# Where the second homes of the activations begin: a shift of 32 columns instead of 48

## What is computed

```python
def mixer(h, hc, lp, rope, n_rows, need_ctx):
    f, nq, nk, nv, cq, ckv, kr, g = jnp.split(h @ lp['w_in'], IN_OFFSETS, axis=-1)
    ...
    out = merge_branches([y_f, y_na, y_mla], g, lp['w_branch'], lp['w_out'])
def swiglu(h, w_gate, w_up, w_down):
    return (jax.nn.silu(h @ w_gate) * (h @ w_up)) @ w_down
def sq_relu_mlp(h, w1, w2):
    u = jax.nn.relu(jnp.einsum("bsd,df->bsf", h, w1))
    return jnp.einsum("bsf,fd->bsd", u * u, w2)
```

## Time and profile before

| | us |
|---|---|
| median of 3 runs | 2148.93 |
| lowest, highest | 2146.88, 2150.05 |
| profiled execution | 2151.08 |
| its span, first to last instruction | 2149.2 |
| TensorE busy | 1972.9 |
| VectorE busy | 1300.5 |
| ScalarE busy | 847.9 |
| GpSimd busy | 138.9 |

### The profile page before, as it was taken

How to read it: one execution, slowest core, us unless ns; L and a number is a source line. 1 busy time by engine, 2 the same in 40 slices (tenths; PEclk the granted TensorE clock), 3 DMA queues, 4 the chain that set the end, 5 groups by cost and what they waited for, 6 DMA issues and landing times.

```text
span 2149.2 us, 31676 instructions
## 1 busy us (share of the span) xinstructions
PE 1972.9 (92%) x12304; PEld 1616.3 (75%) x12304; DVE 1300.5 (61%) x2152; ACT 847.9 (39%) x1364; POOL 138.9 (6%) x118
## 2 busy tenths in 40 slices
PE   4999989999988999999699898989997789988998
PEld 2776657646667788888578483779996789987998
DVE  5422464564447567768733557576667877777765
ACT  4422253253124222222523444454445754444444
POOL 0000000000030000303000000020111300000000
PEclk9999999999999999999899799999998899999999
DMA  8642512204552565565454240666552446653653
GB/s 303 207 137 79 176 40 79 64 1 161 192 172 97 182 212 180 189 202 192 150 196 157 79 142 1 232 212 204 196 192 92 140 148 206 194 165 99 196 188 125
DMA packets 280756, 332.04 MB, mean 154 GB/s; under 512 B 13190, under 2 KB 229692, under 8 KB 280508
## 3 DMA queue, kind: packets, MB, share of 16 engines
q1 hardware_dynamic: 268608, 323.05, 45.5%
q10 hardware_dynamic: 12028, 7.32, 1.3%
HBM read 329.31 MB, written 1.05 MB: 154 GB/s over the span
## 4 chain that ended last, share of the span: by engine, by line
PE 75%; DVE 9%; issue 5%; DMA 5%; ACT 4%; POOL 1%; SPq 1%; ACTq 0%; DVEq 0%; POOLq 0%
PE ps L546 20%; PE ps L547 19%; PE ps L548 19%; PE ps L1269 3%; PE ps L1295 2%; DVE SL L507 2%; PE ps L367 2%; PE ps L1279 2%; DMA RAW<-in_w_in 2%; DMA RAW<-in_w_out 1%; ACT SH L501 1%; PE ps L1504 1%; DMA EARLY<-in_w_mod 1%; DVE RSTD L988 1%; DMA RAW<-in_w_branch 1%
## 5 line engine op out<-in xcount | busy, mean ns | idle before, releaser
L507 DVE TENSOR_TENSOR SL<-RAW,SH 128x1024 fp32r<-128x1024 f32 (+2 forms) x448 | 524.8, 1175 | 439.1 <-ACT SH L501 434.5
L546 PE MATMUL ps<-AB,SH 128*128 128x256 f32 (+1 forms) x1984 | 648.5, 327 | 62.7 <-DVE AB L1008 45.2
L547 PE MATMUL ps<-AB,SH 128*128 128x256 f32 (+1 forms) x1984 | 641.3, 323 | 0.0
L548 PE MATMUL ps<-AB,SL 128*128 128x256 f32 (+1 forms) x1984 | 640.9, 323 | 0.0
L501 ACT ACTIVATE SH<-RAW 128x1024 fp32r<-128x1024 f32 (+2 forms) x448 | 443.1, 997 | 433.1 <-PE ps L548 264.1
L546 PEld LDWEIGHTS ps<-AB,SH 128*128 128x128 f32 x1984 | 382.4, 193 | 114.5 <-issue 59.1
L548 PEld LDWEIGHTS ps<-AB,SL 128*128 128x128 f32 x1984 | 381.0, 192 | 29.7
L547 PEld LDWEIGHTS ps<-AB,SH 128*128 128x128 f32 x1984 | 381.4, 192 | 28.2
L546 PE MATMUL ps<-HH,SH 128*128 128x256 f32 (+1 forms) x992 | 305.8, 308 | 3.2 <-DVE HL L757 1.7
L547 PE MATMUL ps<-HL,SH 128*128 128x256 f32 (+1 forms) x992 | 303.6, 306 | 0.0
L548 PE MATMUL ps<-HH,SL 128*128 128x256 f32 (+1 forms) x992 | 303.5, 306 | 0.0
(11 more groups left out here) (283 smaller groups left out, 2208.8 us busy)
## 6 DMA issues: line engine op xcount, KB each, us to landing
SIDE<-in_w_mod SPq DMA_DIRECT2D x45, 2048.0 KB, 7.9
RAW<-in_ffn_w SPq DMA_DIRECT2D x64, 1024.0 KB, 5.3
RAW<-in_w_in SPq DMA_DIRECT2D x44, 1024.0 KB, 6.2
RAW<-in_w_ffn_gate SPq DMA_DIRECT2D x22, 1024.0 KB, 9.1
RAW<-in_w_ffn_up SPq DMA_DIRECT2D x22, 1024.0 KB, 5.2
RAW<-in_w_ffn_down SPq DMA_DIRECT2D x16, 1024.0 KB, 5.6
RAW<-in_w_branch SPq DMA_DIRECT2D x24, 512.0 KB, 3.4
RAW<-in_w_out SPq DMA_DIRECT2D x8, 1024.0 KB, 7.4
```

The costliest lines, as they stand in the source:

```text
L507: e.tensor_tensor(SL[:, m, 0:kt, :], RAW[p][:, 0:kt, o:o + P], SH[:, m, 0:kt, :].bitcast(F32), ALU.subtract).then_inc(K.up("weight_low"), 1)
L546: e.matmul(ps, SH[:, m, k, :], xh, start=k == 0, stop=False)
L547: e.matmul(ps, SH[:, m, k, :], xl, start=False, stop=False)
L548: ins = e.matmul(ps, SL[:, m, k, :], xh, start=False, stop=k == self.kt - 1)
```

## The change

The constant SHIFT goes from 48 to 32 columns. The second homes of AB, YB, Y8, HH and HL begin 64 bytes earlier than before, at a multiple of 256 bytes in each partition; before, at 64 bytes past one. The first homes, all allocations and all instructions stay.

```diff
 C_ID, C_COS, C_SIN, C_WIN, C_ROT, C_SEL = 0, 128, 384, 640, 704, 736
 C_KEEP = 768
-SHIFT = 48
+SHIFT = 32
 C_DFT = C_KEEP
```

## The result

The median rises from 2147.9 us (2145.6 to 2150.1, four runs) to 2171.0 us (2168.5 to 2172.8, four runs): ratio 1.0101, interval 1.0073 to 1.0128. The change makes the kernel about 23 us slower where 8.7 us of gain were forecast. The profiled execution took 2168.51 us, with a span of 2166.7.

What follows compares the result with a forecast made beforehand. The kernel was taken as bound by how fast TensorE's matmuls follow each other. Slow stretches -9.5 us, waits +0.8, all else 0, make -8.7 from 2148.9, say 2140 us; 8-in-10 range 2136 to 2182.

Steps and rivals of the forecast that it cites:

- What bounds the kernel: Whole kernel: bound by how fast TensorE's split-product matmuls follow each other; TensorE busy 92%, holding 75% of the chain.
- parts 3 and 4: VectorE and ScalarE writes into second homes, then issue, DMA and semaphores: cost nothing, with 693 ns for either home's write.
- part 2: 3 x 48 matmuls of 512 columns in the second home: between -0.9 and +0.9 us, taken as 0.
- part 1: 6624 matmuls of 256 columns in second homes: slow stretches of 248.4 us go at the fast pace, -9.5 us.
- part 5: Values of layer 1 and pooling mix, second home stationary: some 96 matmuls, at most 0.5 us either way.
- reserve for waits: Shorter streams between waits: 0.8 us of the gain taken off, as some would come back as waiting.
- the mechanism that the forecast chose: Second-home streams: toll of two meeting readers vanishes at distance 128, all at 113.1 ns; -8.7 us, chance 0.40.
- sign of a meeting: Weight loads of L546: 192 ns instead of 188 shows matmul and load meeting in SBUF; 188 when nothing meets.
- Repeats every 128 bytes: Second-home streams: distance 128 acts as 0, giving 120 ns; +32 us, 2181 us, chance 0.23.
- The slow pace becomes the rule: Second-home streams: all fall into 117.5 ns; +18 us, 2167 us, chance 0.14.
- Both states stay: Second-home streams draw fast or slow anew: -5 to +6 us, 2144 to 2155 us; 0.20 jointly with no effect.
- The pace doesn't hang on the address: All matmul streams: the change does nothing, 2149 us; chance 0.20 jointly with streams drawing either pace anew.

Runs made afterwards that it cites:

- map1: Separate kernel of bare three-matmul streams at the kernel's buffer addresses, activations or weights moved by 16 bytes at a time: 113.3 to 120.0 ns per 256-column matmul.
- map2: Bare streams of 256 columns, weights fixed, activations moved by one column (4 bytes) over 64 columns: column 27 120.0, 28 113.3, 29 121.8 ns.
- shift0: SHIFT 0 instead of 48 in the kernel before the change, so second homes fall on the first: 2169.7 against 2150.0 us, ratio 1.0088.
- map4: Bare streams with high and low activation halves at different columns (117.5 to 122.2 ns), then both at 28 or 32 with 384 to 128 columns (176.0 to 111.7 ns).
- relw: SHIFT 0 and weight halves 64 bytes higher, distance -64 in all layers, against the kernel before the change: 2160.8 against 2150.0 us, ratio 1.0048.
- shift16: SHIFT 16 instead of 48 in the kernel before the change, second homes at distance +64 from the weights: 2163.7 us, ratio 1.0066.

## Why the prediction was wrong, point by point

*What bounds the kernel* was right: the chain is the same, the whole loss lies in the pace of TensorE, and that a pace must be read from starts was what made it visible at all. *Writes, issue, DMA (parts 3 and 4)* were rightly put at nothing: 692 against 693 ns, the same waits. *512 columns (part 2)* were rightly put at 0: their long streams in layer 1 take 233.3 ns a step in both kernels. (The 9.5 us of part 1 is a slip of a tenth: 248.4 x 0.038 is 9.4.) *Values (part 5)*: 26 steps in 3.09 us, 118.8 against 118 ns, so some 0.1 us.

**The step that failed is the pace in part 1**, the forecast's sentence that the toll is "greatest with both at the same position (120), less and not always at 64 (113 or 118), and gone at 128". It drew a line through three distances to a fourth that no row showed. The table of map1 has no such line: 120 at 0, 113.3 at 112, 118.7 at 128, and map2 shows jumps of 8 ns between neighbours. The size of the term by the right pace is 2110 x 0.9 + 4510 x 5.4 ns less a tenth = 23.8 us, and 2148.9 + 23.8 = 2172.7 against 2171.0 measured; so the counts and the sum held for this kernel, only the one number put into them didn't. They don't hold in general: the same sum gives some 31 us for shift0, whose time rose by 0.88%, 19 us. The reserve for waits could be checked as well. From the 4501st matmul on the span is 21.9 us longer: the steps within the streams take 24.2 us more, and the longer steps between and at the start of streams 2.4 us less. (TensorE's listed busy time there grows by 26.6 us and its idle time shrinks by 4.7; the starts are the safer count, as the ends of matmuls are modelled.) The first 4500 matmuls, which the change doesn't touch, took 4.5 us less in this execution.

The range of 2136 to 2182 us held the 2171.0 only because it took in the rivals' slow ends; the mechanism that the forecast chose had 2136 to 2144.

**The sign of a meeting was misread.** 192 against 188 ns of a load was taken as two readers of SBUF in each other's way, and 188 as the sign that nothing meets. After has 188 ns at 118.7 ns; shift0 has 192 in all three lines at 120; map4 has 192 in the short streams at 111.7. The mean duration of a load doesn't tell the pace.

*The rivals.* "Repeats every 128 bytes" (2181) is refuted by map1. "The slow pace becomes the rule" (2167) had the right shape, one pace for all, and was 1.2 ns short, since it took the slowest pace of the same form, where the true one was a third, new pace. "Both states stay" fell for this distance, since after has one; at -64, where both occur, relw shares 5106 of 6076 groups with the kernel before, more than blind draws with these shares would give (some 55%), though a few long streams make up most of them, and less than a mix fixed by the distance would. "The pace doesn't hang on the address" fell with shift0, shift16 and after. Above all the forecast gave 0.40 to an exact pace for an unseen distance where rows had three distances and three answers. All the slow paces (118, 119, 120) had the same standing by the rows, and map2 shows that a column taken blindly gets 113.33 in both its streams once in 64.

The Trainium skill, page "SBUF — State Buffer", section "Who interferes with whom", says that "PE and ACT never wait on anyone". The traces agree as far as other engines go: the paces are the same with VectorE at work in the MLP loops and at rest in map1. Within TensorE it may have a bound: relw and shift0 have their activations at the same addresses and differ in where the weights stand, and their first MLP stretches go at 113.3 and 120.0 ns. Whether that difference is a wait of one of TensorE's two reads for the other, no run shows. The Trainium skill, page "TensorE: Matmul & The Clock Gate", section "Back-to-back issue gap", gives 109.2 ns for 256 columns and by the same formula 215.8 for 512, as the gap of matmuls by themselves; the lowest seen in these streams, with a weight load for each matmul, are 113.33 and 226.67.

**What is settled and what stays open.** Settled: the pace of fp32r streams of 256 columns hangs on how activations and weights stand to each other; TensorE alone makes it; it belongs to the stream and not to the matmul; with the weights where this kernel has them, 128 bytes is a slow distance and 112 a fast one; the longer steps in the streams (24.2 us) account for the loss of some 23 us. Open: whether two reads meet at all, and if so which and where. No run took the load away, and the rule behind the 64 columns of map2 wasn't found, so a fast column can be measured but not computed. Why +64 draws the slow and -64 mostly the fast of the same two paces in the kernel is open as well, and so is how much of a pace's loss reaches the time: nearly all here (21.9 of 24.2 us), less in shift0 (24.0 of 31.8).

## What to carry to other kernels

Where TensorE is bound by streams of 256 float32 columns, the start of the activations relative to the weights is worth up to 8.5 ns a matmul between neighbouring columns, here 28 us between the best and the changed kernel. It is to be measured column by column on bare streams with both sides at their real addresses: for 256 columns these had the kernel's pace among theirs at all five distances tried there (0, 64, 112, 128, 192). It is never to be interpolated or rounded to a neat multiple: activations at a multiple of 256 bytes (distance 128) had 118.7 ns and at the weights' own position 120, against 113.3 at 112 bytes. And the time can keep less than the steps lost, as in shift0. A slow pace can't be seen in idle time, in the chain or in a mean duration: only in starts, or in a window's length by its count.

## What the runs showed of the hardware that was not expected

- Columns 28 and 29, four bytes apart: 113.33 and 121.8 ns. Among 64 starts the slowest in both streams is column 1 with 123.3, and one stream of column 2 had 126.7.
- 226.67 ns for 512 columns were reached at distance 0 alone, where 256 columns have one of their slow paces (120.0): the best place for one form isn't the best for the other, and relw paid 10.8 us for that.
- Weight loads of 128 columns never followed each other faster than every 111.7 ns in the mean of a stream, and streams of 128 and of 192 columns cost as much as one of 240 at its best (111.8): below some 240 columns a matmul with a load of its own got no cheaper here.
- Streams settle: after some uneven steps the gaps repeat. At distance 112 every gap is 113 or 114 ns, at 0 every one 120, and at 128 they go round in fives, 115, 118, 122, 120, 119, in all four stream kernels alike. A cycle of five in a code whose own cycle is three is one more sign of a rhythm that isn't the program's.
